# Rotary turning of queries and keys in a fused decoder kernel: partition transfers on raw tiles, sine and cosine products first, root factors last

## The reference

```
z = xn @ w_in
zq, zk, zv, hq, hf, hi, hg, u, zg = jnp.split(z, SPLIT_POINTS, axis=-1)
q = rope(rmsnorm(zq.reshape(B, T, SWA_HEADS, SWA_HEAD_DIM), q_norm), pos)
k = rope(rmsnorm(zk.reshape(B, T, SWA_KV_HEADS, SWA_HEAD_DIM), k_norm), pos)

def rmsnorm(x, w):
    y = xf * lax.rsqrt(jnp.mean(xf * xf, axis=-1, keepdims=True) + EPS) * w

def rope(x, pos):
    x1, x2 = xf[..., : hd // 2], xf[..., hd // 2:]
    return concatenate([x1 * cos - x2 * sin, x2 * cos + x1 * sin], axis=-1)
```

## Time and profile before

| | |
|---|---|
| median of 3 runs (lowest, highest) | 950.02 us (949.9, 950.58) |
| the profiled execution | 949.91 us |
| its span, first to last instruction | 948.1 us |
| TensorE busy | 943.3 us (99%), 7944 instructions |
| VectorE busy | 669.3 us (71%) |
| ScalarE busy | 483.8 us (51%) |
| GpSimd busy | 43.2 us (5%) |
| moved by DMA | 164.25 MB, mean 173 GB/s |

### The profile page before, as it was taken

The page is one execution under the profiler, slowest core; times in us unless marked ns, Lnnn a source line. Parts: engine busy times, 40 slices in busy tenths (PEclk is TensorE's granted clock), DMA queues, the critical chain, the costliest instruction groups (busy, mean ns, idle before and its releaser), DMA issues.

```text
span 948.1 us, 18976 instructions
## 1 busy us (share of the span) xinstructions
PE 943.3 (99%) x7944; PEld 914.9 (96%) x7944; DVE 669.3 (71%) x1052; ACT 483.8 (51%) x707; POOL 43.2 (5%) x61
## 2 busy tenths in 40 slices
PE   9999999999999999999999999999999999999998
PEld 8999898999999999999999998989999999999998
DVE  6798798858876755555757887889498676556463
ACT  6429663473664353535553586436537644435351
POOL 0070000000000000000001500000000000000000
PEclk9999999999999999999999999999999999999999
DMA  9655444444554585455475563534444546555542
GB/s 361 219 186 172 184 145 134 135 134 152 156 182 153 192 300 176 156 172 161 162 253 164 189 219 113 166 123 147 135 145 156 182 147 244 172 163 172 160 155 91
DMA packets 44276, 164.25 MB, mean 173 GB/s; under 512 B 4992, under 2 KB 6528, under 8 KB 43648
## 3 DMA queue, kind: packets, MB, share of 16 engines
q1 hardware_dynamic: 42912, 152.95, 49.1%
q0 software_dynamic: 1136, 9.83, 2.7%
q10 hardware_dynamic: 144, 0.26, 0.1%
HBM read 153.29 MB, written 10.29 MB: 173 GB/s over the span
## 4 chain that ended last, share of the span: by engine, by line
PE 97%; DMA 1%; ACT 0%; SPq 0%; DVE 0%; issue 0%; DVEq 0%; ACTq 0%
PE pz L413 90%; PE pm L413 6%; DMA raw<-in_w 1%; PE pm L579 1%; ACT w_hi L783 0%; DVE arena L1022 0%; PE pm L632 0%; PE pm L642 0%; SPq L356 0%; SPq L350 0%; PE pm L531 0%; SPq L360 0%; DVE arena L1054 0%; DVE xp L1058 0%; ACT rstd L801 0%
## 5 line engine op out<-in xcount | busy, mean ns | idle before, releaser
L413 PE MATMUL pz<-a_hi,w_hi 128*128 128x288 f32 x1376 | 413.2, 300 | 0.9 <-DVE a_lo L1027 0.6
L413 PE MATMUL pz<-a_lo,w_hi 128*128 128x288 f32 x1376 | 405.9, 295 | 0.0
L413 PE MATMUL pz<-a_hi,w_lo 128*128 128x288 f32 x1376 | 404.8, 294 | 0.0
L783 ACT ACTIVATE w_hi<-raw 128x1024 fp32r<-128x1024 f32 x266 | 278.0, 1052 | 208.5 <-PE pz L413 196.7
L1013 DVE TENSOR_TENSOR w_lo<-raw,w_hi 128x1024 fp32r<-128x1024 f32 x266 | 327.4, 1231 | 10.8 <-ACT w_hi L783 10.8
L413 PEld LDWEIGHTS pz<-a_hi,w_hi 128*128 128x128 f32 x1376 | 257.9, 187 | 10.5 <-issue 8.6
L413 PEld LDWEIGHTS pz<-a_hi,w_lo 128*128 128x128 f32 x1376 | 259.0, 188 | 0.0
L413 PEld LDWEIGHTS pz<-a_lo,w_hi 128*128 128x128 f32 x1376 | 258.3, 188 | 0.3
L413 PE MATMUL pz<-h_hi,w_hi 128*128 128x288 f32 x768 | 228.2, 297 | 0.0
L413 PE MATMUL pz<-h_lo,w_hi 128*128 128x288 f32 x768 | 226.5, 295 | 0.0
L413 PE MATMUL pz<-h_hi,w_lo 128*128 128x288 f32 x768 | 225.8, 294 | 0.0
(11 more groups left out here) (175 smaller groups left out, 539.9 us busy)
## 6 DMA issues: line engine op xcount, KB each, us to landing
raw<-in_w SPq DMA_DIRECT2D x267, 512.0 KB, 3.5
arena<-in_s SPq DMA_DIRECT2D x2, 2048.0 KB, 9.6
out_ss_out<-arena POOLq DMA_DIRECT2D x2, 2048.0 KB, 8.1
out_u_out<-arena POOLq DMA_DIRECT2D x2, 864.0 KB, 6.8
arena<-arena SPq DMA_DIRECT2D x8, 180.0 KB, 3.2
arena<-in_kcT SPq DMA_DIRECT2D x2, 512.0 KB, 6.9
arena<-in_vc SPq DMA_DIRECT2D x2, 512.0 KB, 7.6
out_kc_out<-in_kc_kept POOLq DMA_DIRECT2D x1, 992.0 KB, 7.0
```

The source lines that it names most:

```text
L413: return nc.tensor.matmul(out, a, b, start=start, stop=stop, **kw)
L783: act_fn(w_hi[:, r], raw[:, r], ACT.Copy).then_inc(s["w_hi"], 1)
```

## The change

The root factor is the same for both halves of a head, so the exchange of the halves, the cosine and the sine can be applied to the raw tiles, and the root multiplied at the end. The norm weight differs between the halves, so the parameters get a second, turned copy of it (`qw_turned`, `kw_turned`).

- SyncE exchanges the halves of the raw tiles, behind unit 11's load instead of unit 13's, when tile 4 has been read.
- VectorE, step 5: raw tiles x norm weight x cosine into `cos_t`, two instructions of 1152 and 288 elements. Step 6: exchanged tiles x turned weight x sine, also two.
- Step 7: the sum, 1440 elements, then times the roots from PSUM in three instructions (1080, 72, 288), which give the rotated `qk`. Steps 9 and 10 have nothing of this any more.
- What waited for `qk_rope` on TensorE, GpSimd and SyncE now waits for `qk_norm`.

```diff
-for _name, _n in (("norm_next", KT), ("norm_ffn", KT), ("qw", 1), ("kw", 1), ("sink", 8), ("sink_s", 1),
+for _name, _n in (("norm_next", KT), ("norm_ffn", KT), ("qw", 1), ("kw", 1), ("qw_turned", 1), ("kw_turned", 1),
+                  ("sink", 8), ("sink_s", 1),
...
+        cos_t = A[:, 5 * T:10 * T]
...
-                    if u == 13:
-                        sp.wait_ge(s["qk_norm"], 3 * l + 3)
+                    if u == 11:
+                        sp.wait_ge(s["z_read_dve"], read_dve(l, U_K))
                         sp.sem_inc(s["sp_passed"], 1)
                         for r in range(0, P, 32):
                             o = r + 32 if r % HD == 0 else r - 32
...
                 if u == 11:
-                    pe.wait_ge(s["qk_rope"], l + 1)
+                    pe.wait_ge(s["qk_norm"], 3 * l + 3)
                     pe.wait_ge(s["v_tok"], 2 * l + 2)
...
             def attention(l, u):
+                if u in (5, 6):
+                    src, turned, table, done = ((qk, "", cos, "qk_cos"), (sin_t, "_turned", sin, "qk_sin"))[u - 5]
+                    dst = cos_t if u == 5 else sin_t
+                    if u == 5:
+                        dve.wait_ge(s["z_read_dve"], read_dve(l, U_K))
+                        dve.sem_inc(s["dve_passed"], 1)
+                        dve.wait_ge(s["cos_sin_landed"], 16 * (l + 1))
+                    else:
+                        dve.wait_ge(s["qk_turned"], 64 * (l + 1))
+                    stt(dst[:, 0:4 * T].rearrange("p (j t) -> p j t", j=4), src[:, 0:4 * T].rearrange("p (j t) -> p j t", j=4),
+                        pr(l, "qw" + turned), bc(table, 4), ALU.mult, ALU.mult).then_inc(s[done], 1)
+                    stt(dst[:, 4 * T:5 * T], src[:, 4 * T:5 * T], pr(l, "kw" + turned), table, ALU.mult,
+                        ALU.mult).then_inc(s[done], 1)
                 if u == 7:
+                    dve.wait_ge(s["qk_cos"], 2 * l + 2)
+                    dve.wait_ge(s["qk_sin"], 2 * l + 2)
+                    tt(cos_t, cos_t, sin_t, ALU.add).then_inc(s["qk_turn"], 1)
                     dve.wait_ge(s["consts_rest"], 16)
+                    dve.wait_ge(s["qk_turn"], l + 1)
+                    dve.sem_inc(s["dve_passed"], 1)
                     dve.wait_ge(s["qk_spread"], l + 1)
-                    q3 = qk[:, 0:3 * QR].rearrange("p (b n) -> p b n", b=3)
-                    stt(q3, q3, pr(l, "qw"), pm[:, 0:3, 0:QR], ALU.mult, ALU.mult).then_inc(s["qk_norm"], 1)
-                    for a, b, w in ((3 * QR, 4 * T, "qw"), (4 * T, 5 * T, "kw")):
-                        stt(qk[:, a:b], qk[:, a:b], pr(l, w), PM[3][:, a - 3 * QR:b - 3 * QR], ALU.mult,
-                            ALU.mult).then_inc(s["qk_norm"], 1)
-                    dve.wait_ge(s["qk_norm"], 3 * l + 3)
-                    dve.wait_ge(s["cos_sin_landed"], 16 * (l + 1))
-                    q5 = qk.rearrange("p (j t) -> p j t", j=5)
-                    tt(qk_rs.rearrange("p (j t) -> p j t", j=5), q5, bc(cos, 5), ALU.mult).then_inc(s["qk_cos"], 1)
-                if u == 9:
-                    dve.wait_ge(s["qk_turned"], 64 * (l + 1))
-                    turned = sin_t.rearrange("p (j t) -> p j t", j=5)
-                    tt(turned, turned, bc(sin, 5), ALU.mult).then_inc(s["qk_sin"], 1)
-                if u == 10:
-                    dve.wait_ge(s["qk_sin"], l + 1)
-                    dve.wait_ge(s["qk_cos"], l + 1)
-                    tt(qk, qk_rs, sin_t, ALU.add).then_inc(s["qk_rope"], 1)
+                    tt(qk[:, 0:3 * QR].rearrange("p (b n) -> p b n", b=3), cos_t[:, 0:3 * QR].rearrange("p (b n) -> p b n", b=3),
+                       pm[:, 0:3, 0:QR], ALU.mult).then_inc(s["qk_norm"], 1)
+                    for a, b in ((3 * QR, 4 * T), (4 * T, 5 * T)):
+                        tt(qk[:, a:b], cos_t[:, a:b], PM[3][:, a - 3 * QR:b - 3 * QR], ALU.mult).then_inc(s["qk_norm"], 1)
```

More of the change, by code:

```diff
@@ L393, in _ @@
                 sp.sem_inc(s["sp_passed"], 1)
-                sp.wait_ge(s["qk_rope"], l + 1)
+                sp.wait_ge(s["qk_norm"], 3 * l + 3)
                 sp.sem_inc(s["sp_passed"], 1)
@@ L1471, in _ @@
                 chain(nc.gpsimd.memset(q_samp, 0.0))
-                pool.wait_ge(s["qk_rope"], l + 1)
+                pool.wait_ge(s["qk_norm"], 3 * l + 3)
                 pool.wait_ge(s["u_front"], l + 1)
@@ L1574, in _params @@
             np.tile(d["q_norm"][l], 2)[:, None], np.tile(d["k_norm"][l], 2)[:, None],
+            *(np.tile(np.roll(np.asarray(d[k][l]), HD // 2), 2)[:, None] for k in ("q_norm", "k_norm")),
             np.tile(sink[None], (P, 1)), np.tile(np.repeat(sink, TS), 4)[:, None],
```

## The result

| | before | after |
|---|---|---|
| median of 6 runs (lowest, highest) | 950.06 us (949.9, 950.58) | 955.44 us (954.67, 956.03) |
| the profiled execution, its span | 949.91 us, 948.1 us | 955.25 us, 953.5 us |

The account below looks back on a forecast made before the run. TensorE, busy 943.3 us of a 948.1 us span, was taken as the bound. The terms summed to 0.0 us on a median of 950.02, giving 950.0; the range ran from 0.2 us below 949.4 up to 951.3.

Parts of the forecast that it names:

- the three rivals: TensorE waiting at the value transposes (953.3 us, 0.04), shifted addresses slowing matmuls (952.7, 0.01), relieved score path (948.0, 0.02).
- the wait at the transposes: Behind unit 9, TensorE waits for late norm products: up to 3.25 us, measurable chance 0.04; smaller waits counted as no change.
- the slower matmuls: Rival on TensorE's matmuls: operands at shifted addresses cost 0.42 ns each, 2.7 us in all, 952.7; chance 0.01.
- The places that were costed at nothing: Cosine products, transfers, step 7, steps 9 and 10 and layer 1: each forecast to cost or gain 0.
- TensorE's two demands: Layer 0: value transposes at 42.74 us, 1.07 us of room; unit 11's low weight half at 46.27, 2.95 us.
- I take 4.6: Landing time in us of the four transfers, the median of nine weight loads; landing at 33.9 us in layer 0.
- the bound of 9.9: Upper bound in us on the transfers' landing time, from the slowest weight load of the trace, issued at 14.57 us.
- the first rival: Landing at L delays the value transposes by L + 1.65 - 36.53, less 1.07; up to 3.25 us, 953.3; chance 0.04.
- the shifted addresses: Rival: activations 32 bytes higher slow 6432 matmuls by 0.42 ns each, 2.7 us, 952.7; decisive from 0.3 ns; chance 0.01.
- That row: Earlier trace's eight 360-column matmuls, slices 1440 bytes apart: two times, one per pass, not per slice; used against the address rival.
- The port rule: GpSimd's first copy could lock the shared port and hold VectorE's split 11 up to 1.12 us; forecast unmoved.
- the row for copies: Earlier trace: VectorE's split at 49.10 us took 1.22 us beside a GpSimd copy, so copies hold split 11 for nothing.

Follow-up runs that it names:

- e3: Changed kernel with 96 unused bytes ahead of the activations and the value transposes behind unit 10 instead of 9: 950.09 us, ratio 1.0004 against the kernel before.
- e2: Changed kernel with 96 unused bytes ahead of the activations, so they start at a multiple of 128 again: 951.68 us, ratio 1.0021 against the kernel before.
- e4: Kernel before with 32 unused bytes behind the activations, ahead of the constants and the arena: 949.79 us, ratio 1.0000.
- e8: Kernel before with everything 32 bytes higher, weights and activations together: 949.93 us, ratio 0.9999.
- e1: Kernel before with 32 unused bytes ahead of the activations, no instruction changed: 951.91 us, ratio 1.0027.
- e12: Changed kernel with only the value transposes put behind unit 10, activations still 32 bytes off: 953.23 us, ratio 1.0033 against the kernel before.
- e5: Kernel before with 64 unused bytes ahead of the activations: 943.81 us, ratio 0.9934.
- e10: Kernel before with w_hi and w_lo 64 bytes higher, activations on their old raster of 128: 943.84 us, ratio 0.9936.
- e9: Changed kernel with 32 unused bytes ahead of the activations (64 off) and the value transposes behind unit 10: 944.21 us, ratio 0.9940 against the kernel before.
- e11: Kernel before with the activations 96 bytes higher: 943.99 us, ratio 0.9937.

## Why the prediction was wrong

The likeliest case, no change, did not come. The mechanisms of two of the three rivals came together: the wait at the transposes, but in a size that the prediction still counted as no change, and the slower matmuls, which alone were worth more than twice the 1.9 us that it called measurable.

*The sum from the order of work.* The places that were costed at nothing did cost nothing: cosine products in the gap (30.4 to 32.3 us), root products the same, earlier scores and GpSimd work without gain. e3 is that sum alone, and it is 1.0004. The count of TensorE's two demands and the choice of the transposes as the one with least room were right.

*The step that failed first: "I take 4.6", the landing of the transfers.* It took up to 7.3 us in layer 0, between my 4.6 and the bound of 9.9. The formula of the first rival held: with L = 36.97 it gives 36.97 + 1.65 - 36.53 - 1.07 = 1.02 us, and unit 9 took 1.08 us more. Its 1.65 us for the two products was worked out wrongly and did little harm: the rows named (1.25 us for 1080 elements, 1.58 for 1440) give 0.92 us per 1000 elements and 0.26 fixed, so 1.84 for both, and the two took 1.76 (37.02 to 38.78). I took a median over a stretch in which the traffic was falling, and took no account that the four transfers are traffic themselves, 720 KB together, behind a 512 KB load on engines at 1.00. The load ahead of them took 6.5 us instead of 4.5. In layer 1, where I expected a landing by about 501, they landed in 4.3 to 5.6 us, and VectorE waited 0.6 us there too; that cost TensorE nothing.

*The step that failed by more: the shifted addresses, given 1 chance in 100.* They cost 4.39 us of the 5.4. I had the mechanism's place and its decisive price (0.3 ns a matmul; measured 26.6 / 24 = 1.1 ns in 165 units of 268, where the rival had reckoned with 0.42 ns in all), and dismissed it by the earlier trace rows. That row could not speak on it. It shows durations of eight small matmuls that run beside each other on parts of the array, in plain fp32, not the distance between the starts of full ones; and their four moving slices, 1440 bytes apart, lie at four different distances from their weights modulo 128 bytes, where all of a unit's lie at one. A duration also says little here: of the changed kernel's unit matmuls, the median rose from 295 to 298 ns only, while their starts moved from 133.3 to 134.4 ns apart. The kernel before, then the changed one (min/median/max in ns):

```profile
L413 PE MATMUL pz<-a_lo,w_hi x1376: 290/295/298, 6.8 to 919.4; 128*128 128x288 f32 x197
```
```profile
L415 PE MATMUL pz<-a_lo,w_hi x1376: 291/298/301, 6.8 to 924.5; 128*128 128x288 f32 x197
```

*The port rule.* GpSimd's copies now stand beside split 11, and the split was not held, as the row for copies said. Its rows, GpSimd's first, then VectorE's:

```profile
44.07 0.28 POOL L1489 COPY arena<-arena 64x128 f32<-64x128 f32 x1 [19.19 <-DVE arena L1087]
44.52 1.11 POOL L1489 COPY arena<-arena 64x128 f32<-64x128 f32 x1 [0.16 <-POOL arena L1489]
```
```profile
44.26 1.21 DVE L1015 TENSOR_TENSOR w_lo<-raw,w_hi 128x1024 fp32r<-128x1024 f32 x1
```

But I had read that row for the wrong engine. The split started first, and it is the copy that waited: a copy of the same form took 0.28 us just before, this one 1.11, and it ended 0.16 us behind the split. GpSimd's spans are rough, but in the profiles of all runs each copy that starts while a split runs ends 0.14 to 0.16 us behind it. The pair in the earlier trace rows is the same (split from 49.10 to 50.32, copy from 49.34 to 50.46). So the Trainium skill's rule (SBUF — State Buffer, "SBUF: two separate sides"), that the later of the two waits out the other, agrees with this pair. It agrees with the long split of the earlier trace rows too, beside this addition of GpSimd, in the kernel before:

```profile
64.09 1.08 POOL L1500 TENSOR_TENSOR arena<-arena 128x417 f32<-128x417 f32 x1
```

The split started at 64.35, when 0.83 us of the addition were left, and lasted 1.91, which is 1.08 more. No wait of TensorE comes from either.

The range ended at 951.3 because it held a small wait only. With the two slow rivals added at their upper ends (3.25 and 2.7 us) it would have reached 956, and would then have held the result in part by luck, since the 2.7 us stood on 0.42 ns a matmul in all units and not on 1.1 ns in 165 of them.

## What to carry to other kernels

Where one engine is full, cost the memory layout as part of a change: two more columns a layer in one tensor moved every tensor behind it and cost four times what the reordering cost. Fix the start addresses of the two matmul operands to each other and pin them with explicit padding (here 64 and 96 bytes modulo 128 were best), so that an edit elsewhere can't move them. When a transfer is moved to an earlier place, take its landing time from the busiest row there and add its own bytes, and put what waits for it behind work that TensorE needs soon, or give TensorE's next demand more room.

## What the runs showed of the hardware

The pace of the 128 x 128 by 288-column fp32r matmuls, each with its own weight load, depended on the distance between the starts of the moving and the stationary tensor, modulo 128 bytes: at 0, 3.200 us for 24 (the kernel before, e2, e3, e4, e8); at 32, 3.200 or 3.227, in runs (changed kernel, e1, e12); at 64 and 96, 3.173 (e5, e10, e9, e11). Other distances were not run. Between e5 and e12, the fastest kernel and the slowest without a wait at the transposes, lie 9.4 us of some 950, with the full clock granted in both and nothing in the tables of waits to explain it. The slices inside the tensors lie 1152 and 512 bytes apart, both multiples of 128, so that one distance holds for all of them.

The Trainium skill (SBUF — State Buffer, "SBUF: two separate sides") says that TensorE never waits on another engine for its port. The runs don't contradict it, since both operands are TensorE's own. That the two streams, weight loads and moving operand, meet in the memory is the plainest reading of a pace that hangs on their distance alone, but no run watched the memory itself.
